# A two-block, four-layer float32 network on one core: fewer bank waits at the head of each feed-forward, its first tokens taken through both up units together, and an earlier split of the second weight chunk

## The reference, cut to what matters

```python
mod = c_act @ ada_w[layer] + ada_b[layer]                # 6 vectors of 1024
sh_m, sc_m, gt_m, sh_f, sc_f, gt_f = jnp.split(mod, 6)
x = x + gt_m * mixer(...)
h = rms_norm(x, g) * (1 + sc_f) + sh_f
# block 1, layer 0: dense    f = (silu(h @ w1) * (h @ w3)) @ w2            (1024 x 2816, twice, 2816 x 1024)
# block 1, layer 1: experts  top 2 of 8 by h @ router_w, then the same form for each expert
# block 2, both layers:      u = causal_conv3(h @ w_up) + b;  f = (gelu(u[:2816]) * u[2816:]) @ w_down
x = x + gt_f * f
```

## Time and profile before

| what | value |
|---|---|
| median of 3 runs (lowest, highest) | 2212.55 us (2207.90, 2221.78) |
| profiled execution, first to last instruction | 2208.6 us |
| time of the profiled execution outside that span | not listed apart |
| busy: PE, PE weight load, DVE, ACT | 2139.0, 1923.3, 1749.7, 1228.3 us |
| dense feed-forward begins | 167.44 us |
| router begins, experts begin | 482.13 us, 505.11 us |
| conv feed-forwards begin | 1554.83 us, 2001.93 us |

### The profile page before, as it was taken

How to read it: one execution, slowest core, us unless ns; L and a number is a source line. 1 busy time by engine, 2 the same in 40 slices (tenths; PEclk the granted TensorE clock), 3 DMA queues, 4 the chain that set the end, 5 groups by cost and what they waited for, 6 DMA issues and landing times.

```text
span 2208.6 us, 33379 instructions
## 1 busy us (share of the span) xinstructions
PE 2139.0 (97%) x13865; PEld 1923.3 (87%) x13865; DVE 1749.7 (79%) x1903; ACT 1228.3 (56%) x1367; POOL 54.0 (2%) x101
## 2 busy tenths in 40 slices
PE   6999999999999999999999999999999999999998
PEld 5989999987888888888888898888899998888998
DVE  5998777868899998989899977777667677756665
ACT  3724444736777777766767754641455455324554
POOL 1000000000000000000000000000000000000000
PEclk8999999989999999999999999999999999999999
DMA  9887985647999999999999967737455376345552
GB/s 318 314 309 279 330 312 187 224 153 290 378 379 360 370 375 367 361 371 378 367 367 378 373 208 202 260 121 280 144 187 186 101 208 197 97 133 172 172 189 79
DMA packets 339039, 578.55 MB, mean 262 GB/s; under 512 B 48098, under 2 KB 208954, under 8 KB 326594
## 3 DMA queue, kind: packets, MB, share of 16 engines
q1 hardware_dynamic: 324604, 475.34, 62.9%
q0 software_dynamic: 13824, 100.67, 11.7%
q10 hardware_dynamic: 454, 0.34, 0.1%
HBM read 575.26 MB, written 1.05 MB: 261 GB/s over the span
## 4 chain that ended last, share of the span: by engine, by line
PE 81%; DVE 10%; ACT 4%; DMA 3%; issue 2%; DVEq 0%; ACTq 0%; POOL 0%; POOLq 0%
PE bank L597 80%; ACT arena L1572 2%; DVE w_low L2117 2%; DMA ada_in<-in_ada_w 2%; DVE ada_acc L2125 1%; DVE arena L2125 1%; DMA ring<-in_moe_w 1%; DVE arena L2117 1%; PE bank L1331 1%; DVE arena L2611 1%; ACT L1572 1%; ACT mix_hi L1572 1%; DVE h L2125 0%; DVE x L2125 0%; DVE arena L2589 0%
## 5 line engine op out<-in xcount | busy, mean ns | idle before, releaser
L2117 DVE TENSOR_TENSOR w_low<-ring,moe_w_hi 128x2048 fp32r<-128x2048 f32 x264 | 594.4, 2286 | 12.7 <-ACT moe_w_hi L1572 8.6
L1572 ACT ACTIVATE moe_w_hi<-ring 128x2048 fp32r<-128x2048 f32 x264 | 506.4, 1919 | 168.8 <-DMA ring<-in_moe_w 123.9
L597 PE MATMUL bank<-h_hi,w_hi 128*128 128x256 f32 x1056 | 260.9, 285 | 10.8 <-ACT h_hi L1572 5.8
L597 PE MATMUL bank<-h_hi,w_low 128*128 128x256 f32 x1056 | 260.2, 283 | 0.0
L597 PE MATMUL bank<-mix_h_hi,mix_hi 128*128 128x256 f32 x800 | 230.4, 291 | 10.6 <-ACTq L1569 7.4
L597 PE MATMUL bank<-mix_h_hi,w_low 128*128 128x256 f32 (+2 forms) x848 | 238.0, 284 | 0.0
L597 PE MATMUL bank<-h_low,mix_hi 128*128 128x256 f32 x800 | 213.8, 283 | 0.0
L597 PEld LDWEIGHTS bank<-h_hi,w_hi 128*128 128x128 f32 x1056 | 201.0, 190 | 13.0 <-issue 6.9
L2125 DVE SCALAR_TENSOR_TENSOR ada_acc<-ada_in,c_col,ada_acc 128x2048 f32<-128x2048 f32 x84 | 197.2, 2347 | 15.8 <-DMA ada_in<-in_ada_w 10.9
L597 PEld LDWEIGHTS bank<-h_hi,w_low 128*128 128x128 f32 x1056 | 202.3, 192 | 0.0
L1572 ACT ACTIVATE arena<-bank 128x512 f32<-128x512 f32 (+2 forms) x171 | 90.2, 527 | 192.2 <-PE bank L597 188.4
(11 more groups left out here) (219 smaller groups left out, 4577.5 us busy)
## 6 DMA issues: line engine op xcount, KB each, us to landing
ring<-in_moe_w SPq DMA_DIRECT2D x264, 1024.0 KB, 6.5
ada_in<-in_ada_w POOLq DMA_DIRECT2D x96, 1024.0 KB, 7.5
ring<-in_w_in SPq DMA_DIRECT2D x56, 1024.0 KB, 5.7
ring<-in_ffn_w_up SPq DMA_DIRECT2D x44, 1024.0 KB, 7.7
ring<-in_ffn_w SPq DMA_DIRECT2D x33, 1024.0 KB, 8.1
ring<-in_ffn_w_down SPq DMA_DIRECT2D x22, 1024.0 KB, 4.9
ring<-in_w_out SPq DMA_DIRECT2D x16, 1024.0 KB, 5.4
ring<-in_w_br_mla SPq DMA_DIRECT2D x4, 1024.0 KB, 5.1
```

The costliest lines, as they stand in the source:

```text
L597: ins = nc.tensor.matmul(out, lhsT, rhs, start=start, stop=stop, skip_group_check=shared)
L1572: return nc.scalar.activation(out, in_, f, **kw)
L2117: return nc.vector.tensor_tensor(out, a, b, op)
```

## The change

Four edits, no arithmetic added or removed.

1. In `ffn_modulation`, and in DVE's matching `modulation` calls, the last modulation of the dense and the expert layer goes to bank 2 instead of bank 0.
2. `ffn` on PE waits for banks 0 and 1 before block 0 and for banks 2 to 7 before block 1. `moe_route` waits for bank 0 ahead of the router and for banks 1 to 7 ahead of the transposes.
3. Block 0's products up go token-block-wise, `kb` by `kb`, through both units (4 matmuls for each `h_ready`), then the `h_low` products in the same interleaving.
4. Chunk 1 is split earlier: unit 0 ahead of block 0's first work on ACT and DVE, unit 1 on ACT between block 0's SiLU or taps and what follows, on DVE behind `hidden_low` of block 0.

```diff
@@ ffn_modulation (PE) @@
-                fill(0)
-                modulation(0, 5 * KB, MODS)
+                fill(2)
+                modulation(2, 5 * KB, MODS)
@@ new on PE @@
+            def up_first(slots, b):
+
+                units = [(w, w_hi[w].rearrange("p (k f) -> p k f", k=KB),
+                          w_low[:, slots[w], :].rearrange("p (k f) -> p k f", k=KB)) for w in range(2)]
+                for kb in range(KB):
+                    need("h_ready")
+                    for w, hi, low in units:
+                        mm(bank[b + w][:, 0:T], hi[:, kb, 0:P], h_hi[:, kb, :], start=(kb == 0), stop=False)
+                        mm(bank[b + w][:, 0:T], low[:, kb, 0:P], h_hi[:, kb, :], start=False, stop=False)
+                for kb in range(KB):
+                    need("h_lo")
+                    for w, hi, low in units:
+                        mm(bank[b + w][:, 0:T], hi[:, kb, 0:P], h_low[:, kb, :], start=False,
+                           stop=(kb == KB - 1), inc="up_done" if w and kb == KB - 1 else None)
...
@@ ffn (PE) @@
-                for b in range(8):
-                    fill(b, readers=b // 4)
                 for f in range(FFN_FB + 1):
+                    for b in ((0, 1), (2, 3, 4, 5, 6, 7))[f] if f < 2 else ():
+                        fill(b, readers=b // 4)
...
-                        up_split(c, [plan[k][0] for k in keys], fb2, 2 * (f % 2), first=(f == 0))
+                        slots = [plan[k][0] for k in keys]
+                        if f == 0:
+                            up_first(slots, 0)
+                        else:
+                            up_split(c, slots, fb2, 2 * (f % 2))
@@ moe_route (PE) @@
-                for b in range(8):
-                    fill(b, readers=0)
                 fill(0)
...
                 assert not owed
 
+                for b in range(1, 8):
+                    fill(b, readers=0)
@@ conv_ffn (ACT); ffn (ACT) alike, around its SiLU @@
+                split_high("u", li, 1, (0,))
                 for f in range(FFN_FB):
                     down_rows_high("u", li, f, f0)
                     taps(f)
+                    if f == 0:
+                        split_high("u", li, 1, (1,))
                     gelu(f)
                     hidden_high(f, f0)
-                    if f % 2 == 0:
+                    if f and f % 2 == 0:
 
                         split_high("u", li, f // 2 + 1)
@@ conv_ffn (DVE); ffn (DVE) alike @@
+                split_low("u", li, 1, (0,))
                 for f in range(FFN_FB):
                     down_rows_low("u", li, f, f0)
                     taps(f)
...
                     if f % 2 == 0:
-                        split_low("u", li, f // 2 + 1)
+                        split_low("u", li, f // 2 + 1, (0, 1) if f else (1,))
@@ the DVE program @@
-            modulation(0, 5 * KB, MODS, 0)
+            modulation(0, 5 * KB, MODS, 2)
...
-            modulation(1, 5 * KB, MODS, 0)
+            modulation(1, 5 * KB, MODS, 2)
```

More of the change, by code:

```diff
@@ L1166, in mixer2 @@
                     project(("wout2", li, j), b, KB, hk, 2, per_kb=None if j else "ycat_ready", inc="wout_psum")
-            def up_split(chunk, slots, fb2, b, first=False):
+            def up_first(slots, b):
[11 more added lines that the diff above has]
+                           stop=(kb == KB - 1), inc="up_done" if w and kb == KB - 1 else None)
@@ L1171, in up_split @@
+            def up_split(chunk, slots, fb2, b):
                 cols = slice(fb2 * P, (fb2 + 1) * P)
                 his = [w_hi[(2 * chunk + w) % 4].rearrange("p (k f) -> p k f", k=KB) for w in range(2)]
-                def high(w):
+                for w in range(2):
+                    out = bank[b + w][:, 0:T]
                     low = w_low[:, slots[w], :].rearrange("p (k f) -> p k f", k=KB)
                     for kb in range(KB):
-                        if first and w == 0:
-                            need("h_ready")
-                        mm(bank[b + w][:, 0:T], his[w][:, kb, cols], h_hi[:, kb, :], start=(kb == 0), stop=False)
-                        mm(bank[b + w][:, 0:T], low[:, kb, cols], h_hi[:, kb, :], start=False, stop=False)
@@ L1182, in rest @@
-                def rest(w):
+                        mm(out, his[w][:, kb, cols], h_hi[:, kb, :], start=(kb == 0), stop=False)
+                        mm(out, low[:, kb, cols], h_hi[:, kb, :], start=False, stop=False)
                     for kb in range(KB):
-                        if first and w == 0:
-                            need("h_lo")
-                        mm(bank[b + w][:, 0:T], his[w][:, kb, cols], h_low[:, kb, :], start=False,
+                        mm(out, his[w][:, kb, cols], h_low[:, kb, :], start=False,
@@ L1187, in rest @@
                            stop=(kb == KB - 1), inc="up_done" if w and kb == KB - 1 else None)
-                high(0)
-                if not first:
-                    rest(0)
-                high(1)
-                if first:
-                    rest(0)
-                rest(1)
             def down_split(slot, fb2, n, w_hi2, first, last):
@@ L1619, in rope, with split_high @@
                 act.sem_inc(s["rope_ready"], 1)
-            def split_high(kind, li, chunk):
+            def split_high(kind, li, chunk, units=(0, 1)):
                 if chunk < CHUNKS:
-                    for w in range(2):
+                    for w in units:
                         slot, count, _ = plan[(kind + "13"[w], li, chunk)]
```

8 lines of the change are left out of this document (6 added, 2 removed).

## The result

| | median us (lowest, highest) | runs | profiled execution: time, span |
|---|---|---|---|
| before | 2209.45 (2207.90, 2221.78) | 7 | span 2208.6 |
| after | 2198.30 (2195.71, 2201.34) | 7 | 2195.71, span 2193.9 |

The ratio of after to before is 0.994, with an interval of 0.9925 to 0.9954 (the two medians alone give 0.995). The forecast was 2200 us, "0.57% less", and its range of 2192 to 2210 us had a chance of 0.90.

A forecast was written before the change was run, and what follows sets the result against it. PE bounds the kernel (busy 97% of the span), so only its gaps or low-clock stretches can pay. 5.1 x 2 + 0.9 + 1.5 = 12.6 us, from the median 2212.55 to 2199.95, said as 2200 us; range 2192 to 2210.

The forecast's parts named there:

- The conv heads: Both conv feed-forwards: PE starts 2.4 us earlier at full clock, down 0 at 1564.95; 5.1 us gained each, at least 1.4.
- The rival of the slow clock: Conv heads: PE starts early but stays at 1.2 GHz, or ACT's longer order delays GELU; 2207 us, chance 0.12.
- The router: Router: PE starts at 480.6 instead of 482.13, its 32 matmuls taking 6.26 us; 1.5 us gained.
- upper bound of 1.58: Router: bounds of the gain put at 0 and 1.58 us; PE's gap there was 1.58.
- The dense head: Dense feed-forward: PE starts at 166.55 instead of 167.44; 0.9 us gained, bounds 0 and 0.95.
- the second rival: Dense head and router pay nothing because a DMA-timed wait ends those stages; 10.2 us left, 2202 us, chance 0.10.
- SP and POOL issue the same transfers in the same order: Whole kernel, among costs taken as nothing: the transfers issued by SP and POOL keep their order.
- The statement that the early split costs nothing: Dense feed-forward: of 3.5 us, earlier start takes 0.9 and the split ahead on DVE at most 2.25, leaving 0.35.
- The interleaving: Block 0's products up over two banks: changes neither weights nor shapes, cost taken as nothing.
- up 0 ends at 1558.1: First conv feed-forward: PE starts at 1552.4 and up 0 takes 5.66 us at full clock.
- ACT 0.75 us before GELU: First conv feed-forward: ACT's table load ends at 1562.35, and GELU isn't wanted before 1563.1.
- The experts: Experts, as a rival: shifted start costs DMA pace; 0.3 us later per unit gives 2239 us, chance 0.05.

The follow-up runs named there:

- banks-only kernel: The kernel before with only edits 1 and 2, the bank waits; old order of block 0 and old split of chunk 1: 2202.10 us, ratio 0.9964.
- split-only kernel: The kernel before with only edit 4, the early split of chunk 1; old bank waits and old order: 2210.40 us, ratio 1.0006.
- the order undone: The change without edit 3, so block 0 goes unit by unit in the old order: 2199.86 us, ratio 0.9956.
- the dense split late: The change with edit 4 undone in the dense feed-forward alone, chunk 1 split behind block 0 there: 2197.03 us, ratio 0.9934.
- thin `ada_in`: The change with layer 1's ada loads cut to an eighth of their columns, later modulation stale: 2195.49 us, one run.
- best: The change with dense split late and, in the first conv feed-forward alone, early w2 rows and both chunk 1 units rounded before the taps: 2195.65 us, ratio 0.9934.
- the run with `keep_busy` alone: The kernel before with only more `keep_busy` matmuls ahead of the conv feed-forwards, router and dense head: 2208.47 us, ratio 0.9994.
- early rows: The change with block 0's w2 rows split during the norm's sum and both chunk 1 units rounded before the taps, both conv feed-forwards: 2197.36 us, ratio 0.9937.
- best with more `keep_busy`: The best kernel plus `keep_busy` matmuls ahead of the router's rank sums (one) and gathering (two): 2195.65 us, ratio 0.9933.
- thin `ada_in`, before: The kernel before with layer 1's ada loads cut to an eighth of their columns, later modulation stale: 2219.95 us, one run.

## Why the prediction was right, and where it was not

**The conv heads** came out by the mechanism and by the size: 4.95 and 4.99 us against 5.1, with the start, the clock and the start of down 0 each where they were put. The two parts tried apart, banks (up 2 at 18.31 us after `h_hi`) and split (19.43 in the second conv feed-forward), gained 2.8 and 1.7 us of head time, 4.5 together. The rival of the slow clock fell: in the seven profiled executions with both edits and no further one at the second head (the change twice, the order undone, the dense split late, thin `ada_in`, both best ones) every window of 2 us from the first product up to 20 us behind it reads 1.00 at both heads.

**The router** was the mis-sized term: 3.66 us against 1.5. The start came 1.75 us earlier, near the 1.5. The working left the 32 matmuls at 6.26, though I had just priced the same effect at the conv heads, and they gave the other 1.91. The earlier trace rows give 0.196 us for each of them; the windows there read 0.72 and then 0.50, and I had not opened them. Without the gap they take 3.63 us in five of nine executions and 4.08 to 4.74 in the others. The run with `keep_busy` alone gains 2.63 us with the start unmoved, 2.55 of them in the 32 matmuls. The forecast's upper bound of 1.58 was therefore wrong too.

**The dense head** is where the second rival came true, for one of its two places: 1.28 us were won by up 2, more than the 0.9 of the working, and given back at up 6 and up 10 by waits that are timed by DMA. The prediction had said "against: no such wait on PE". It had looked at PE's waits and at the order of the issues, which did not change, and not at their spacing, which did: "SP and POOL issue the same transfers in the same order" is true and was not enough. The statement that the early split costs nothing failed for four of its five profiled executions with whole `ada_in` pieces, by 1.7 to 4.0 us behind the head. All five show ACT's wait at block 2, and none with the late split does; in the fifth the wait is 1.39 us and costs nothing. Beside the late split the change's stretch is 1.4 us longer (203.55 against 202.17), in one execution each, and the medians of the two can't be told apart.

**The interleaving**, taken as nothing, is worth 0.55 us at each conv head, so the gain was in the sum without its cause. The step "up 0 ends at 1558.1" needs it. The working left ACT 0.75 us before GELU; the trace shows 0.34, and the old order ends block 0 0.90 later, which leaves 0.56 to pay.

**The experts** were no rival in the end. ACT's waits for `in_moe_w` within their first 750 us were 118.5 us in 129 and are 120.2 in 134 (502 to 1252 us), and the stretch moved by -2.5 us. Over all thirteen executions it lies between 1044.1 and 1047.0, and the change itself has 1044.17 once and 1046.05 once, so this is what one execution differs from the next. It can account for most of what sets the profiled difference (14.7) above that of the medians (11.15).

The traces show two parts of it. In the first 10 us of the experts the granted clock is 1.00 and PE has 43 matmuls in three executions (before, the change's first, early rows). It is 0.83 with 36 or 37 in nine others, and 0.70 with 32 in the last kernel; lined up matmul by matmul, the nine are then 1.4 to 1.6 us behind and that one 2.6. So the change's first profile was a lucky one. Against the kernel before, which has the full clock there too, it gains by shorter waits of PE: 0.9 us in one for `arena` and 0.3 in one for `w_low`, where there were 2.3 in three and 1.1. Why these vary was not tried.

**The first conv stretch of the kernel with the dense split late** is 443.57 us, 1.4 longer behind the same head. Lined up with the change, its PE is level to 0.02 us until the clock falls to 0.50 in the mixer behind, at 1818.12 us, and 1.43 to 1.45 late from there on. So it is the clock, and not the edit.

## What to carry over

Price a pause of PE twice, the idle time and the matmuls behind it at the low clock, and open the clock windows at every place whose pause the change touches, not only at the longest. When work is moved earlier on an engine that also frees DMA buffers, look at when the freed transfers start against the others: an unchanged order with another spacing can give the gain back. And where two profiles differ by 1 or 2 us in a stretch that no edit touches, line them up matmul by matmul and look at the clock before looking for a cause in the kernel.

## What the runs showed of the hardware

- **Short pauses and the clock.** Behind each pause of 2.88 us the clock fell to 0.50. Behind those of 2.04 to 2.06 us it fell in three places and held in five: in the banks-only kernel it fell in the first conv feed-forward and held in the second. At the end of the first mixer PE pauses in every kernel; it held there behind 1.42 to 1.55 us in six executions, 1.79 (dense split late) and 1.83 (best), and fell behind 1.72 (split only), 1.90 (thin `ada_in`, before) and 2.19 (no interleaving, early rows, best with more `keep_busy`). So the length of the pause alone does not decide. Behind 0.46 at the conv heads and 0.65 at down 0 it always held. The Trainium skill ("TensorE: Matmul & The Clock Gate", Part 1) says that the number of slow matmuls differs from run to run with the phase of the hardware's own counting; these executions agree as to the difference and cannot show the cause.
- **The clock can fall without a pause.** In the change PE works through from the modulation to the transposes, and yet loses its clock among the router's matmuls of 8 columns. All nine executions without the gap lose it there or in the transposes behind:

```profile
481.00:483.00 2.00, 2.00 (x19) 1.87 (x17) 1.73 (x6) 2.00 (x6) 0.00 (x0) 1.00 0.00 0
483.00:485.00 2.00, 2.00 (x16) 2.00 (x16) 0.00 (x0) 2.00 (x3) 0.00 (x0) 0.75 0.03 8
485.00:487.00 2.00, 2.00 (x10) 2.00 (x11) 1.07 (x6) 2.00 (x3) 0.00 (x0) 0.50 0.00 0
```

In the mixer of the kernel with the dense split late it falls as well, and PE has no gap there either:

```profile
1818.00:1820.00 2.00, 2.00 (x12) 2.00 (x11) 1.78 (x4) 1.64 (x3) 0.00 (x0) 0.53 1.15 406
```

- **Small matmuls pay it too.** The 32 of them take 3.63 us at full clock and 6.26 in the kernel before, a factor of 1.7, though they stream only 8 columns each. In the split-only kernel, where the clock is at 0.50 for nearly all of them, they take 6.83.
- **A table load is behind, not beside.** GELU's load took 1.28 us in the rows above; the Trainium skill ("ScalarE: Activation LUTs", What ACT_TABLE_LOAD costs) gives about 1283 ns, and adds a drain of some 1380 ns, of which the trace shows nothing: with the old order the load starts 0.02 us behind ACT's work before it, and GELU 0.01 us behind the load.
